# Hybrid GLA and differential attention layer on one Trainium2 core: the first norm's weights on a DMA queue of their own, and another order of the first twenty microseconds

## The reference, cut to what matters

```python
def rmsnorm(x, w):
    xf = x.astype(jnp.float32)
    y = xf * lax.rsqrt(jnp.mean(xf * xf, axis=-1, keepdims=True) + EPS)
    return (y * w.astype(jnp.float32)).astype(x.dtype)
...
    h = rmsnorm(x, norm_mix_w[l])
    proj = h @ w_in[l]
    gq, gk, gv, ggate, ga, dq, dk, dv, dgate = split_cols(proj)
    g_logit = (ga @ w_alpha2[l] + b_alpha2[l]).astype(f32)
```

## Time and profile before

| what | value |
|---|---|
| median of 3 runs (lowest to highest) | 828.2 us (828.14 to 828.29) |
| the profiled execution's own time | 828.41 us |
| its span, first to last instruction | 826.7 us |
| PE busy | 814.4 us, 99% of the span |
| DVE, ACT, POOL busy | 586.1, 435.6, 83.7 us |
| chain that ended last | 92% PE, 4% DVE, 1% ACT, 1% DMA |
| granted TensorE clock | 0.998, 9 tenths or more in all 40 slices |

### The profile page before, as it was taken

The page is one execution under the profiler, slowest core; times in us unless marked ns, Lnnn a source line. Parts: engine busy times, 40 slices in busy tenths (PEclk is TensorE's granted clock), DMA queues, the critical chain, the costliest instruction groups (busy, mean ns, idle before and its releaser), DMA issues.

```text
span 826.7 us, 13231 instructions
## 1 busy us (share of the span) xinstructions
PE 814.4 (99%) x4586; PEld 683.9 (83%) x4586; DVE 586.1 (71%) x1360; ACT 435.6 (53%) x1057; POOL 83.7 (10%) x123
## 2 busy tenths in 40 slices
PE   8999999999999999999999999999999999999996
PEld 7888888888788888888888898888888888888885
DVE  6788677776578678767857878599835464367997
ACT  6875445454455345435545676544645454366443
POOL 3100121210010011111100000010010000001201
PEclk9999999999999999999999999999999999999999
DMA  8321359962233345645412268855422121206945
GB/s 289 115 83 39 102 179 199 186 132 66 62 108 109 88 79 108 130 86 116 102 61 84 61 211 262 265 148 128 134 96 72 45 65 43 85 13 139 215 93 203
DMA packets 70409, 99.21 MB, mean 120 GB/s; under 512 B 6596, under 2 KB 38472, under 8 KB 70344
## 3 DMA queue, kind: packets, MB, share of 16 engines
q1 hardware_dynamic: 52360, 64.29, 24.4%
q0 software_dynamic: 15392, 29.36, 19.8%
q10 hardware_dynamic: 2592, 4.72, 1.8%
HBM read 83.68 MB, written 31.46 MB: 139 GB/s over the span
## 4 chain that ended last, share of the span: by engine, by line
PE 92%; DVE 4%; ACT 1%; DMA 1%; issue 1%; SPq 0%; ACTq 0%
PE bank L1849 14%; PE bank L1851 14%; PE bank L1850 14%; PE banks2to L1849 10%; PE banks2to L1851 10%; PE banks2to L1850 10%; PE banks6to L1921 4%; PE banks2to L2121 3%; PE bank L2144 2%; DVE neg_max L1648 2%; PE bank L2146 1%; PE banks6to L2081 1%; DVE w_lo L1387 1%; PE banks6to L1851 1%; PE banks6to L1849 1%; PE banks6to L1850 1%
## 5 line engine op out<-in xcount | busy, mean ns | idle before, releaser
L1851 PE MATMUL bank<-w_hi,actT_lo 128*128 128x512 f32 x412 | 161.3, 391 | 0.0
L1849 PE MATMUL bank<-w_hi,actT_hi 128*128 128x512 f32 x384 | 156.6, 408 | 0.3
L1850 PE MATMUL bank<-w_lo,actT_hi 128*128 128x512 f32 x384 | 149.9, 390 | 0.0
L1387 DVE SCALAR_TENSOR_TENSOR w_lo<-w_raw,vecs,w_hi 128x512 fp32r<-128x512 f32 x120 | 86.6, 748 | 27.2 <-ACT w_hi L1105 27.1
L1851 PEld LDWEIGHTS bank<-w_hi,actT_lo 128*128 128x128 f32 x412 | 77.4, 188 | 16.9
L1849 PEld LDWEIGHTS bank<-w_hi,actT_hi 128*128 128x128 f32 x384 | 72.2, 188 | 18.0 <-DVE w_lo L1387 1.5
L1105 ACT ACTIVATE w_hi<-w_raw,vecs 128x512 fp32r<-128x512 f32 x120 | 82.5, 719 | 7.7 <-DMA w_raw<-in_w_in 4.1
L1850 PEld LDWEIGHTS bank<-w_lo,actT_hi 128*128 128x128 f32 x384 | 72.4, 189 | 12.6
L991 POOL TENSOR_TENSOR rs_o<-var_o,neg_half 128x1 f32<-128x1 f32 (+1 forms) x48 | 29.0, 604 | 375.6 <-DVE var_o L1675 256.8
L1851 PE MATMUL banks2to<-w_hi,actT_lo 128*128 128x512 f32 x164 | 64.0, 390 | 0.0
L1270 ACT ACTIVATE prob<-banks2to,neg_maxs 128x128 f32<-128x128 f32 (+7 forms) x64 | 46.9, 740 | 15.1 <-DVE neg_maxs L1649 15.0
(11 more groups left out here) (372 smaller groups left out, 2043.9 us busy)
## 6 DMA issues: line engine op xcount, KB each, us to landing
w_raw<-in_w_in SPq DMA_DIRECT2D x56, 256.0 KB, 3.4
out_sums<-in_w_out POOLq DMA_DIRECT2D x11, 1024.0 KB, 10.3
late_sums<-in_w_co POOLq DMA_DIRECT2D x11, 1024.0 KB, 9.3
w_raw<-in_w_ckv SPq DMA_DIRECT2D x32, 256.0 KB, 3.5
w_raw<-in_w_cq SPq DMA_DIRECT2D x32, 256.0 KB, 2.8
stage_in<-in_x SPq DMA_DIRECT2D x8, 512.0 KB, 4.4
tile_a<-mixed ACTq DMA_DIRECT2D x16, 256.0 KB, 3.2
x_res<-in_x SPq DMA_DIRECT2D x8, 512.0 KB, 6.3
```

The costliest lines, as they stand in the source:

```text
L1387: return dve.scalar_tensor_tensor(dst, src, scale, hi.bitcast(F32), ALU.mult, ALU.subtract)
L1849: pe.matmul(dst, l_hi, r_hi, start=start, stop=False)
L1850: pe.matmul(dst, l_hi, r_lo, start=False, stop=False)
L1851: return pe.matmul(dst, l_lo, r_hi, start=False, stop=stop)
```

## The change

The mixing norm's weights leave the group of small vectors: ScalarE issues their load as its first instruction, with a semaphore of its own (d_mix), and `vec` turns only them, from rows 0 to 8. The other vectors and the positions are turned by a new stage `vec2`, into bank 2. SP's first DMAs change their order: weight tile 0 goes ahead of input tile 2, and weight tile 1 ahead of input tile 3. The list of stages is rewritten up to `w 2`: `vec` stands among the filler transposes, weight tile 0 is split between the two first scalings, `sq 2` goes behind tr 0, G0h 0 stands ahead of tr 2, G0h 1 between tr 2 and tr 3, and `vec2` between G0h 1 and tr 3. Because `vec2` writes bank 2, which tr 3 fills too, tr 3 waits for its copies. The filler transposes stay 42 in number.

```diff
-    plan = [("zeros",), *normed(0), *normed(1), ("sq", 2), *busy(0, 24), ("tr", 0, 0), ("pos",), ("scale", 2), ("tr", 0, 1)]
-    plan += [*busy(1, 2), ("tr", 1, 0), ("vec",), ("tr", 1, 1), *busy(2, 6), ("sq", 3), ("w", 0), ("tr", 2, 0), ("scale", 3)]
-    plan += [("tr", 2, 1), *busy(3, 10), ("G0h", 0), ("w", 1), *tr(3), ("G0h", 1), ("w", 2), ("const",)]
+    plan = [("zeros",), ("sq", 0), *busy(0, 18), ("vec",), *busy(1, 8), ("scale", 0), ("sq", 1), ("w", 0), ("scale", 1)]
+    plan += [*tr(0), ("sq", 2), *busy(2, 4), *tr(1), ("w", 1), ("scale", 2), *busy(3, 12), ("G0h", 0), ("sq", 3)]
+    plan += [("pos",), ("tr", 2, 0), ("scale", 3), ("tr", 2, 1), ("G0h", 1), ("vec2",), *tr(3), ("w", 2), ("const",)]
...
+        d_mix = sem("mix_norm_loaded")
...
-            for t in range(3):
-                load_input(t)
+            load_input(0)
+            load_input(1)
+            load_weight(0)
+            load_input(2)
             for dst, src in (
-                (vec_rows[0:8, :], a["norm_mix_w"][0].rearrange("(k p) -> k p", p=P)),
...
-            load_weight(0)
+            load_weight(1)
             load_input(3)
-            load_weight(1)
...
+            act.dma_start(vec_rows[0:8, :], a["norm_mix_w"][0].rearrange("(k p) -> k p", p=P)).then_inc(d_mix, 16)
...
                 elif kind == "vec":
                     dve.wait_ge(vec_pe, 1)
-                    then_wait(dve.tensor_copy(vecs[:, :], banks[5][:, 0:28]))
-                    dve.tensor_copy(pos_f[:, :], banks[5][:, 28:36]).then_inc(vec_dve, 1)
+                    dve.tensor_copy(vecs[:, 0:8], banks[5][:, 0:8]).then_inc(vec_dve, 1)
+                elif kind == "vec2":
+                    dve.wait_ge(vec_pe, 2)
+                    dve.tensor_copy(vecs[:, 8:28], banks[2][:, 8:28])
+                    dve.tensor_copy(pos_f[:, :], banks[2][:, 28:36]).then_inc(vec_dve, 1)
...
                 elif kind == "vec":
                     pe.wait_ge(pool_c, 4)
-                    pe.wait_ge(d_vec, 16 * 7)
+                    pe.wait_ge(d_mix, 16)
+                    pe.transpose(banks[5][:, 0:8], vec_rows[0:8, :], ident[0:8, 0:8]).then_inc(vec_pe, 1)
+                elif kind == "vec2":
+                    pe.wait_ge(d_vec, 16 * 6)
                     pe.wait_ge(pos_dve, 1)
-                    pe.transpose(banks[5][:, 0:28], vec_rows[:, :], ident[0:28, 0:28])
-                    pe.transpose(banks[5][:, 28:36], pos_rows[:, :], ident[0:TT, 0:TT]).then_inc(vec_pe, 1)
+                    pe.wait_ge(tr_dve, at("tr", 1, 1))
+                    pe.transpose(banks[2][:, 0:28], vec_rows[:, :], ident[0:28, 0:28])
+                    pe.transpose(banks[2][:, 28:36], pos_rows[:, :], ident[0:TT, 0:TT]).then_inc(vec_pe, 1)
                 elif kind == "tr":
                     t, kk = w
                     pe.wait_ge(scaled, at("scale", t))
                     wait(pe, tr_dve, at(*stage) - 4)
+                    if t == 3:
+                        pe.wait_ge(vec_dve, 2)
```

More of the change, by code:

```diff
@@ L1136, in _ @@
                     act.wait_ge(z_pe, at("z", n))
+                    act.wait_ge(vec_dve, 2)
                     if n:
@@ L1398, in _ @@
                 elif kind == "pos":
-                    dve.wait_ge(d_vec, 16 * 7)
+                    dve.wait_ge(d_vec, 16 * 6)
                     dve.tensor_copy(pos_rows[:, :], pos_i[:, :]).then_inc(pos_dve, 1)
@@ L1408, in _ @@
                     dve.tensor_reduce(lam_s[:, 0:2], lam_pr[:, :, :], AX.X, ALU.add).then_inc(dve_c, 1)
-                    dve.wait_ge(vec_dve, 1)
+                    dve.wait_ge(vec_dve, 2)
                     inv = (THETA ** (-np.arange(0, ROPE, 2, dtype=np.float32) / ROPE)).astype(np.float32)
```

## The result

The changed kernel takes 830.67 us (median of 10 executions, 830.2 to 833.38), the kernel before 828.29 (10, 828.1 to 828.57): a ratio of 1.0034, interval 1.0025 to 1.0044. It is slower by 2.4 us; 829.4 was predicted. Three of its ten executions (831.5, 832.81 and 833.38) had a mean granted clock of 0.994 or 0.995, the others 0.998 or 0.999. The profiled execution took 830.77, with a span of 829.0 against 826.7.

What follows compares the result with a forecast made beforehand. PE was taken to work unbroken from 16 us on, so the start of ga 0 decides: G0h 0 2.2 us earlier, but ga 0 at 19.85 against 18.66, 1.2 later. Added to the median of 828.2: 829.4, range 828.4 to 830.4.

Steps and rivals of the forecast that it cites:

- The steps: Up to ga 0: G0h 0 at 12.2, 2.2 us early, then lost to DVE's order, vec2's copies and tr 3's uncovered way.
- the sum: At ga 0: all steps together put its start at 19.85, 1.2 us later than before.
- 19.85 less 18.66: Start of ga 0 forecast for the changed kernel, less its start in the kernel before: 1.2 us later.
- scaling 3 at 15.57 ... the second lo part at 16.35: On DVE before tr 3: scaling 3 starts at 15.57, tr 2's second lo part at 16.35; 0.78 per scaling.
- its upper bound: Added to the sum: late third tile 0.3, late tr 0 0.2, stretched w_lo or scaling; +0.5, so +1.7 us.
- PE starts about 0.05 behind the DVE operation that it waited for: Hand-over from DVE to PE: 0.05 us taken; 0.15 seen where PE waited for w_lo 0.
- the eight fillers and the turned vector keep PE until about 7.45: On PE ahead of tr 0: it is busy until about 7.45 instead of 7.23.
- the first tile there at 4.3: At the kernel's start: ACT's first square waits for its input tile until 4.3.
- Nothing is given back later: Behind ga 0: no real work ahead of it is left out, so its lateness carries to the end.
- The clock: Rival: PE's clock falls around two stalls of 1.0 and 1.6 us, for 5.6 us; +2.8, 832.2; 6 in 100.
- The small load: Rival: the mixing norm's weights land at 6.8, delaying scaling 0 and tr 0; +1.9, 830.1; 8 in 100.
- DVE's queue: Rival: DVE's order does not bind, ga 0 at 16.7, 2.0 early, 826.2; 5 in 100.

Runs made afterwards that it cites:

- e2: The changed kernel with vec2 moved behind tr 3 and into bank 0, so tr 3 waits for no copies: 829.69 us, ratio 1.0024.
- e3: The changed kernel with scaling 3 put ahead of the lo parts of tr 2: 829.93 us, ratio 1.0026.
- e4: The changed kernel with scaling 3 ahead of tr 2, G0h 1 behind tr 3, then vec2 in bank 0: 827.98 us, ratio 0.9999.
- e5: The changed kernel with only G0h 1 moved back behind tr 3, vec2 staying ahead of tr 3: 831.24 us, ratio 1.0034.
- e6: The changed kernel without the twelve filler transposes ahead of G0h 0: 830.93 us, ratio 1.0037.
- e8: The changed kernel with scaling 3 early, G0h 1 and vec2 behind tr 3, and square 3 and scaling 2 ahead of weight tile 1: 827.65 us, ratio 0.9993.
- p_after: The changed kernel run again unchanged, giving its second profile: 831.89 us, ratio 1.0048.
- b1: The kernel before with only the mixing norm's weights moved to ScalarE's queue: 828.28 us, ratio 1.0.
- e7: The changed kernel with scaling 3 early, G0h 1 and vec2 behind tr 3, and the small load issued by SP: 827.88 us, ratio 0.9995.

## Why the prediction was wrong

It gave 829.4 with a range to 830.4; 830.67 came. The mechanism was the one predicted and its sum was too small, and a rival that was given 6 in 100 came on top.

**The steps held.** G0h 0 came early and brought 2 us, tr 2 came directly behind it, DVE idled for 1.34 us with scaling 3 behind the lo part, tr 3 was released by the copies of `vec2`, ga 0 by the lo parts of tr 3. e2, e3 and e4 show by intervention that scaling 3's place and the copies are worth 0.8 us of the leg each, and that the order of stages holds all of the loss. The third part, the way of tr 3 that G0h 1 no longer covers, is shown only together with the others: e4 gains 0.9 us more than e2 and e3 add up to, and G0h 1 moved back alone (e5) gains nothing.

**The step that failed is the sum.** Three of its terms were too small, and its "19.85 less 18.66" took the kernel before from one trace. ga 0 was 1.95 late, not 1.19; the 0.76 between them splits as follows.
- *"scaling 3 at 15.57 ... the second lo part at 16.35"*: 0.78 from one start to the next, taken from a row in which an operation of POOL that had started first overlapped the scaling by 0.32 us (14.60 and 0.51 of the cast, against 14.79). It was 1.07 (15.83 to 16.90): +0.29. The lo part ahead of it had moved it into POOL's operation of 15.40 to 16.42. The prediction had such a stretch in its upper bound, as a repeat of the earlier trace rows, but not that the move puts it there. The Trainium skill (SBUF — State Buffer, "SBUF: two separate sides") calls the pair of ports of VectorE and GpSimd an exclusive lock that the first to start holds, for some forms of VectorE's operations, while the other fully blocks. The rows agree on who pays: the scaling that started second took 1.14, and 0.74 behind POOL's last operation (e6); the one that started first, in e8, took 0.73 and POOL's cast 1.04, where it takes 0.50 in the changed kernel. They differ on how much: 0.40 and 0.54 us were lost, less than the overlaps of 0.59 and 0.67.
- *"PE starts about 0.05 behind the DVE operation that it waited for"*: 0.15 both times (copies end 17.73, tr 3 17.88; lo parts end 20.46, ga 0 20.61): +0.20. The prediction had seen 0.15 in its own rows and chose the smaller. Small steps in between add 0.04.
- *"the eight fillers and the turned vector keep PE until about 7.45"*: tr 0 started at 7.75, and +0.23 of that reached G0h 0 (12.43, not 12.2). The fillers behind the vector started 0.22 us apart, the pace of the earlier trace rows, and kept tr 0 back 0.2 us longer than scaling 0 did (6.75 and 0.75). In the second profile they got faster midway, tr 0 started at 7.47 and G0h 0 at 12.15, as predicted:

```profile
5.98 1.57 PEld L1936 LDWEIGHTS banks6to<-ident 128*128 128x128 f32 x8
...
5.99 1.11 PEld L1936 LDWEIGHTS banks6to<-ident 128*128 128x128 f32 x8
```

The rows are the weight loads of these eight fillers, in the changed kernel's first profile and in p_after's. The prediction also had the first tile there at 4.3, and it was there at 4.65, but in p_after, with the tile at 4.57, this cost nothing against the sum. Which tile binds did change: in ten of the thirteen profiles with the changed order G0h 0 starts 7.57 to 7.59 us behind the first square (4.43 to 4.85), and 7.66 to 7.78 in the three others, where the fillers ended late; before, it was the third tile's landing.

**"Nothing is given back later"** was off by 0.37 us between the two first profiles: 2.32 late at the end, 1.95 at ga 0. The 0.76 and the 0.37 are the 1.1 us by which the profiled execution (830.77) missed its own forecast of 829.6. The 0.37 belongs to the trace of the kernel before. Its second profile had ga 0 at 18.22; against that one, with the first square at 4.68 and 4.65, ga 0 was 2.39 late and PE ended 2.43 late, as the medians are 2.38 apart. So single traces of one kernel differ by 0.4 us at ga 0, and the prediction gave the 18.66 it subtracted no such width.

**The clock.** The rival had its mechanism right, two stalls with eight transposes between them, and was given too little chance. Of the 20 executions of the changed kernel 13 were low, three of ten in the first set and all ten later; with fillers in the same stalls none of 11 (none of six against all of five on one chip). Its price was 5.6 us at the low level and 2.8 lost: the second profile shows 3.4 us and 1.5, the third 6.8 us and 2.7. The first set's median owes only some 0.3 us to it (the seven others have 830.39), the later ones 1.0 to 1.5. Why the same kernel fell in three of ten in the first set and in all of ten later, on two chips, is open.

**The other rivals.** The small load was not late: PE turned its rows at 5.36 to 5.80, behind the fillers, in every profile in which ScalarE issues it, with no wait for the load, and b1 alone measured 1.0. (Issued by SP in e7, PE did wait 0.58 us for it, until 5.95, and ga 0 was no later for that.) DVE's queue did bind. Nothing came out faster by more than a measurement can tell: in e8, the best order tried, ga 0 is 0.97 and 0.53 ahead of the two profiles of the kernel before, and the median 0.5.

## What to carry to other kernels

When a piece of work is moved ahead of a chain, look at which engine's queue holds the next link: here 2 us of earlier matmuls were paid back, 0.8 us of it because a scaling that was ready stood behind an operation that had become later, and 0.8 because the copies that emptied a bank stood ahead of the work that fills it. Work put back to cover a hand-over (G0h 1 behind tr 3) gained nothing while an earlier wait still held that hand-over. Two kernels of the same median can differ in how often their executions fall to the low clock: short fillers in stalls of one to two microseconds removed that here (1.0 us of the median on one chip), though not the lateness itself.

## What the runs showed of the hardware that was not expected

- The clock fell behind stalls of 1.2 and 1.7 us with only eight transposes between them, in 13 of 20 executions. It fell in 4 of 5 with a further stall of 2 us ahead of them (e6) and in 3 of 5 with one of 2.6 us in their place (e5). The four profiles of such executions show it low for 3.4 us (three) and 6.8 us (one). With the stalls filled with transposes of the identity: 0 of 11.
- The first square, which waits for the first input tile, starts at 4.43 to 4.86 us in all later profiles and at 4.33 in the first of the kernel before, whatever queue the small load is on.
- DVE's scaling of a tile takes 0.74 us alone and 0.86 to 1.15 where an operation of POOL had started before it; where the scaling started first, POOL's cast takes 0.85 to 1.05 instead of 0.50.
- Two executions of some 220 ran far slower as a whole, 1948.82 and 1193.64 us, on the same chip.
